# A hybrid diffusion layer on one core: one early dot in the last head, value blocks ahead of the last gate set, a modulation block behind the first two turns

## What is computed

```python
s1 = jnp.einsum('nhc,hkc->nhk', q[:, :, 0], p['sub_keys'][0]); s2 = ...   # 8 heads, 128 keys each
v1, i1 = lax.top_k(s1, TOPK); v2, i2 = lax.top_k(s2, TOPK)                # TOPK = 16
top_s, pos = lax.top_k(cand, TOPK); idx = ...; gates = softmax(top_s)
act = gelu(einsum('nd,nhkd->nhk', xb, expert_u[ib]))
out = einsum('nhk,nhkd->nd', act * gb, expert_v[ib])
```

## Time and profile before

| | us |
|---|---|
| median of 3 executions | 2940.51 (2938.43 to 2943.66) |
| profiled execution, its time | 2936.83 |
| its span, first to last instruction | 2935.0 |
| PE busy | 2807.2 (96%) |
| DVE busy | 2178.6 (74%) |
| ACT busy | 1224.7 (42%) |
| POOL busy | 968.8 (33%) |

### The profile page before, as it was taken

One profiled execution on the slowest core, in us unless ns is written; L12 is line 12 of the kernel. 1 busy time (PEld: TensorE's weight loads), 2 busy tenths in 40 slices (PEclk: granted clock), 3 DMA queues, 4 the chain that ended last, 5 costly groups with the idle time before them and its releaser, 6 DMA issues.

```text
span 2935.0 us, 59432 instructions
## 1 busy us (share of the span) xinstructions
PE 2807.2 (96%) x24142; PEld 2477.1 (84%) x24142; DVE 2178.6 (74%) x3107; ACT 1224.7 (42%) x1889; POOL 968.8 (33%) x626
## 2 busy tenths in 40 slices
PE   6999999999999989899989999999999999999998
PEld 4999999677777869799989888888888887777776
DVE  3245553666666653579998999988888989999988
ACT  3333333333333343353336666654444434343333
POOL 0001101122222220049883444431114444444442
PEclk8999999799999989999999999999999999999999
DMA  9633332343341045557779999999999999999997
GB/s 404 264 122 129 123 132 77 134 149 121 127 143 67 5 174 182 183 205 268 251 251 339 360 397 395 393 389 417 417 401 418 417 418 418 418 417 418 417 418 311
DMA packets 205973, 813.66 MB, mean 277 GB/s; under 512 B 81328, under 2 KB 99888, under 8 KB 116688
## 3 DMA queue, kind: packets, MB, share of 16 engines
q1 hardware_dynamic: 103312, 525.61, 46.9%
q0 software_dynamic: 36864, 268.45, 22.1%
q10 hardware_dynamic: 65600, 16.78, 2.5%
HBM read 771.45 MB, written 39.32 MB: 276 GB/s over the span
## 4 chain that ended last, share of the span: by engine, by line
PE 25%; DMA 13%; DVE 12%; issue 5%; SPq 1%; ACT 1%; another core or an unknown queue 0%; DVEq 0%; ACTq 0%
DMA work<-act_table 13%; PE ps L2121 12%; PE ps L2126 6%; PE ps L2474 2%; DVE x L2674 2%; DVE work L2800 2%; DVE wlo L2805 2%; DVE ps L2614 1%; DVE ps L2606 1%; DVE work L2608 1%; PE ps L2525 1%; PE ps L2519 1%; PE ps L2518 1%; DVE work L2646 0%; PE ps L2109 0%
## 5 line engine op out<-in xcount | busy, mean ns | idle before, releaser
L2562 POOL DMA_INDIRECT work<-expert_v,idx x128 | 341.2, 2666 | 378.1 <-DVE work L2800 360.6
L2518 PE MATMUL ps<-whi,hboth 128*128 128x512 f32 x1024 | 399.5, 390 | 6.2 <-ACT whi L2329 6.2
L2121 PE MATMUL ps<-hboth,whi 128*128 128x512 f32 x1664 | 403.4, 394 | 0.0
L2519 PE MATMUL ps<-whi,hboth 128*128 128x512 f32 x1024 | 399.3, 390 | 0.0
L2562 POOL DMA_INDIRECT x<-u_rows,idx x128 | 245.5, 1918 | 437.3 <-DVE x L2674 254.7
L2121 PEld LDWEIGHTS ps<-hboth,whi 128*128 128x128 f32 x1664 | 305.2, 188 | 60.5
L2800 DVE SCALAR_TENSOR_TENSOR work<-work,dots 128x2048 f32<-128x2048 f32 x127 | 297.8, 2345 | 2.3 <-DMA work<-expert_v,idx 2.2
L2525 PE MATMUL ps<-wlo,hboth 128*128 128x512 f32 x1024 | 255.7, 392 | 15.3 <-DVE wlo L2805 15.3
L2525 PEld LDWEIGHTS ps<-wlo,hboth 128*128 128x128 f32 x1024 | 190.6, 188 | 62.6 <-DVE wlo L2805 23.6
L268 PE MATMUL ps<-hhi,whi 128*128 128x384 f32 x704 | 236.2, 335 | 0.0
L270 PE MATMUL ps<-hhi,wlo 128*128 128x384 f32 x704 | 235.2, 334 | 0.0
(11 more groups left out here) (425 smaller groups left out, 5977.2 us busy)
## 6 DMA issues: line engine op xcount, KB each, us to landing
raw<-expert_u SPq DMA_DIRECT2D x85, 1024.0 KB, 8.0
work<-expert_v SPq DMA_DIRECT2D x64, 1024.0 KB, 15.0
raw<-expert_v SPq DMA_DIRECT2D x64, 1024.0 KB, 15.0
raw<-w_in SPq DMA_DIRECT2D x50, 1024.0 KB, 4.8
x<-w_ada SPq DMA_DIRECT2D x48, 1024.0 KB, 5.4
raw_more<-expert_u SPq DMA_DIRECT2D x43, 1024.0 KB, 7.8
z<-w_ada SPq DMA_DIRECT2D x42, 1024.0 KB, 10.4
raw<-w_out SPq DMA_DIRECT2D x16, 1024.0 KB, 4.8
```

The lines of the kernel that those rows point to most:

```text
L2121: pe.matmul(both, whi[:, r, k, :], hboth[:, :, k, CTX:T], start=(k == 0), stop=False)
L2518: pe.matmul(bank, ah, vh[:, part], start=first, stop=False)
L2519: pe.matmul(bank, al, vh[:, part], start=False, stop=False)
L2562: nc.gpsimd.indirect_dma_start(out=buf, out_offset=None, in_=rows, in_offset=bass.IndirectOffsetOnAxis(ap=idx[:, s:s + 1], axis=0)).then_i ...
```

## The change

Three places are edited.

1. In the scan pairs the early modulation slot 3 no longer stands ahead of the last score step; it stands behind `turn_first(1)`. ACT's copy of the sums moves behind its copy of the second turned group.
2. In the heads there are 19 early dots in place of 21: head 7 has one in place of three. The scatter stage has 69 in place of 67. POOL issues one gather behind the low part of each of three blocks (m = 9, 10, 11 and so on), where it issued three behind the first.
3. `done_tok` is placed ahead of `vg`, so that it lies under `stage[0]`. SP waits for the stores of `stage[0]` alone, loads the value blocks 0 and 1, and only then waits for the stores of `stage[1]` and loads the first set.

```diff
                 def one(it, more):
-                    ada_copy(it, 0)
                     for g in range(GR):
                         turned.wait(act, it, g + 1)
                         if g == 2:
                             ada_sums(it, 0)
                         tn_ready.inc(nc.scalar.activation(tn[:, g], ...))
+                        if g == 1:
+                            ada_copy(it, 0)
...
                         if n >= 2:
-                            ada(it, n - 2)
+                            if n - 2 < ADA_EARLY - 1:
+                                ada(it, n - 2)
                             scores_masked.wait(pe, it, 2 * n - 2)
...
                     turn_first(0)
                     turn_first(1)
+                    ada(it, ADA_EARLY - 1)
                     scores_masked.wait(pe, it, 12)
...
-        EARLY_DOTS = DOTS_PER_HEAD * (PKH - 1)
+        EARLY_DOTS = DOTS_PER_HEAD * (PKH - 2) + 1
...
         accs = carve(fb_, D)
+        done_tok = carve(fb_, 2, D)
         vg = [carve(fb_, D) for _ in range(4)]
-        done_tok = carve(fb_, 2, D)
...
                 load_fixed(M_DOWN - 1)
+                sp.wait_ge(stage_out[0].sem, 16 * (SETS // 2))
+                load_v(expert_v[0], 0)
+                load_v(expert_v[1], 1)
+                sp.wait_ge(stage_out[1].sem, 16 * (SETS // 2))
                 for r in range(2):
-                    sp.wait_ge(stage_out[r].sem, 16 * (SETS // 2))
                     sp.wait_ge(spilled[r].sem, 16 * 2)
                 groups(0, 0)
-                load_v(expert_v[0], 0)
-                load_v(expert_v[1], 1)
                 groups(1, 2)
...
-                        for s in range(DOTS_PER_HEAD * (h - 1), DOTS_PER_HEAD * h):
-                            pool.wait_ge(idx_ready.sem, s // TOPK + 1)
-                            gather_u(s)
+                    s = DOTS_PER_HEAD * (h - 1) + (m - 1) % PER_HEAD
+                    if 1 <= h < PKH and (m - 1) % PER_HEAD < DOTS_PER_HEAD and s < EARLY_DOTS:
+                        pool.wait_ge(idx_ready.sem, s // TOPK + 1)
+                        gather_u(s)
...
-                    for s in range(DOTS_PER_HEAD * (h - 1), DOTS_PER_HEAD * h):
+                    for s in range(DOTS_PER_HEAD * (h - 1), min(DOTS_PER_HEAD * h, EARLY_DOTS)):
                         dot(s)
```

More of the change, by code:

```diff
@@ L2012, in build_program @@
         accs = carve(fb_, D)
+        done_tok = carve(fb_, 2, D)
+        assert fb_[0] == NK * GT
         vg = [carve(fb_, D) for _ in range(4)]
-        done_tok = carve(fb_, 2, D)
         v_raw = [done_tok[:, r].rearrange("p (k c) -> p k c", k=KD) for r in range(2)] + [raw[:, 0], raw[:, 1]]
```

## The result

The changed kernel takes 2923.25 us (median of 4 runs, 2923.11 to 2927.75) against 2942.09 for the kernel before in the same measurement (4 runs): a ratio of 0.9938, 95% interval 0.9922 to 0.9955. A second measurement on another chip gave 0.9950 (0.9937 to 0.9963). So the change is worth 15 to 19 us. The forecast was 5.7, and the range's lower end, 2927, was not low enough. The two profiled executions are only 13.7 us apart: that of before lies 5.3 us under the median of its four, that of the changed kernel 0.1 under its own.

The account below looks back on a forecast made before the run. PE was taken to set the up stage and DMA bytes the down stage. Edits of -3.4, -2.0 and -0.3 summed to -5.7 us, so 2934.8 us against a median of 2940.5; range 2927 to 2942.

Parts of the forecast that it names:

- Edit 1, -3.4: Scan pairs: PE's 0.57 us wait for the last masks goes in each of six pairs, 3.4 us together.
- PE does the same work in another order: Scan pairs: reordered PE reaches the sums at 630.33, later than the masks, so only its 0.57 us idle time goes.
- Edit 2, -2.0: Heads and scatter stage: gate turns 3.9 us earlier, scatter stage 3.0, less 1 us for dot 19; bounds -8.7 and +4.
- (a): Head 1: the third gather, now behind a later low part, lands late; its dot loses 5 to 7 us on DVE.
- (b): Heads 2 and 3: about half of the contention between dots and POOL's low parts goes, -4 us.
- (c): Heads 4 to 6: the low part meets each third dot, 2.2 us less 0.7 from the first dot; +4.5 us in all.
- rival 1: Head stage gives all it has: PE's 7.6 us wait and 1.1 of its start go; -12.4 us, 2928.1; chance 0.22.
- 2.2 us either way: Heads 4 to 6: a dot meeting a low part costs 2.2 us more, whichever of the two comes first.
- Edit 3, -0.3: Handover to the down stage: bytes bind, only 0.45 us of DMA time to be won; bounds -4 and +6.
- the rival that the store slips beside the value blocks: Handover: the last table store slips and DVE stands at the first set; 2947 in the middle, 2952 at most; chance 0.08.
- Up to 4 us of slip PE's old wait covers: Handover: without ACT's 4.20 us wait the down start is about 2189 against 2193.07, leaving 4 us for a late store.
- lands near 2176: Handover: by the skill's turns rule the last table store lands near 2176 beside the value blocks; Edit 3 would give -0.45.

Follow-up runs that it names:

- h2: The changed kernel with value blocks 2 and 3 also loaded ahead of the wait for the last table store; 2927.0 us, 0.9957 of the kernel before.
- c3: The changed kernel with the last store's first rows stored apart and only 64 of 128 rows in the first two table stores; 2925.7 us, 0.9951 of before.
- c2: The changed kernel with only the first 64 of 128 rows stored in the first two table stores; 2924.0 us, 0.9946 of the kernel before.
- c1: Edits 1 and 2 on the kernel before, with only 64 of 128 rows stored in the first two table stores; 2923.6 us, 0.9943 of before.
- e12_no_handover: Edits 1 and 2 on the kernel before, without edit 3; 2924.9 us, 0.9951 of the kernel before.
- after_again: The changed kernel, all three edits, measured once more; 2925.5 us, 0.9950 of the kernel before.
- e12_again: Edits 1 and 2 without edit 3, measured again beside the changed kernel on one chip; 2923.8 us, 0.9942 of the kernel before.
- e2: Edit 2 alone on the kernel before; 2929.2 us, 0.9962 of the kernel before.
- h1: The changed kernel with the last table store in two, the first gate sets' rows apart with their own semaphore; 2929.3 us, 0.9963 of the kernel before.

## Why the prediction was wrong, point by point

**Edit 1, -3.4: right in its mechanism, too small.** The 0.57 us waits went, in all six pairs. The step that failed is "PE does the same work in another order": the same matmuls cost PE 0.27 us less per pair in the new order. 0.84 x 6 = 5.0 us, which is what the edit alone measured (-5.0); the 6.4 us between the means of the traces hold the variation of the scan stage as well.

**Edit 2, -2.0: this is where the forecast broke.** Its parts can be read from the starts of the first dots, against the 6.1 us by which the heads begin earlier. (a) was a little short: the third dot waits 7.3 us for its gather, and head 2 begins 8.0 late, where the sum had 6. (b), "about half of that contention goes", was too little: heads 2 and 3 take back 3.1 and 3.7 us, where the sum had 4 for both; head 2's first dot, 4.04 us, had been contended as well, and the sum did not count it. (c) failed outright: "the low part follows at once, so that it meets the third dot: 4.48 - 2.28 = 2.2 us in each". It does meet it, and the dot pays nothing, because the dot had begun first. Heads 4 to 6 gave -1.2 us (the first dot of head 4, 2.49 instead of 3.66) and not +4.5. The forecast had +6.5 us for DVE at head 7 where the trace has 0; the turns then came 9.1 us sooner behind the heads' first matmul, not 3.9. The 9.1 are PE's wait (7.63 less 0.72), its waits for POOL's low parts near 1508 (3.0 us before, 1.1 now), and 0.2 in small. Another 1.5 us came behind the turns, where PE's six matmuls take 272 to 300 ns instead of 421 to 448: the granted clock is 1.00 (the upper level) from 1519 to 1539, and was 0.83 in the mean from 1525 to 1545 in the kernel before, where PE had just stood for 7.6 us. That is rival 1 nearly word for word, at 0.22.

By the Trainium skill, "SBUF — State Buffer", section "Who interferes with whom", the two engines exclude each other for a whole instruction, and the prediction worked out -2.1 us for the three heads by that rule, for a low part that comes second, beside its own +4.5. The changed kernel gave -1.2. Its trace and the kernel with the low parts in quarters agree with the rule (3.37 us for a dot that meets 1.30 us pieces). I had a number by which to choose: the low parts of 4.46 us in the earlier trace rows are 2.40 plus nearly a whole dot of 2.28, which turns explain and a shared rate does not explain better; and I took "2.2 us either way".

**What no step had.** Two more gathers in the scatter stage bring the landing of the first table store from 99.9 us to 105 to 120, past the 104.4 us after which its buffer is wanted. The prediction spoke only of the last store, at the handover. Some executions lose 10 us by it.

**Edit 3, -0.3.** That bytes bind the down stage was right, and so was the rival that the store slips beside the value blocks; the 0.08 for it was too low, although the price was not 2947. The slip is 11 us (209.6 to 220.4; 209 to 213 in the traces without edit 3, 219 to 220 in those with it as it stands and without a long wait of ACT). The failed step is "Up to 4 us of slip PE's old wait covers", which looked at PE only. What the slip moves is the DMA work that stands behind the store: on SP's queue the set and value blocks 2 and 3, on POOL's the gathers of value rows (8.8 us). DMA time of 5.9 us was lost where 2.7 was lost before. SP's share is not the whole: in h2 the value blocks stood ahead of the wait and in c3 the sets did not wait for the store either, and 5.7 and 5.0 us were lost all the same, while POOL stood 12.5 and 15.0 us. No run lets POOL go ahead, so its share is argued and not shown. The Trainium skill's rule on turns, from "DMA: Bandwidth & Descriptors", section "Queues, rings and completion order", led me to "lands near 2176"; the store's lateness by 11 us says that turns beside value blocks are slower turns, so the rule gave no bound. By pairs of traces the edit costs 1.4 to 4.0 us from the last up product on (c2 against c1, the edit alone, the changed kernel against e12_no_handover). By the times it costs 3.8 us alone (0.05 to 0.29%), and 0.4 and 1.7 us on top of the others, which these runs can't tell from nothing. In part that is the long wait of ACT: where it delays PE, the last store has landed before it is wanted, and after_again and e12_again take 730.2 and 732.1 us to the end, edit 3 or not. The rest stays open.

**The chances.** Faster by over 0.2% had 0.49 and came out. Two errors of the same sign, in (b) and (c), and the 0.27 of edit 1 outweighed what edit 3 cost and made the sum too small by 8.0 us against the profiled execution (5.7 for 13.7). That alone would have ended at the range's edge: 2936.8 - 13.7 + 3.7 is 2926.8. The rest of the miss is the 3.7 us that the sum added for the median; here the median lay 0.1 above the profiled execution.

## What to carry to other kernels

Where two engines exclude each other, ask which instruction is issued first: the one that is already running loses nothing, and the other waits for all that is left of it. A long instruction on the engine with slack is then the costly one. Cutting it into pieces halved the price of one meeting here, from 2.2 to 1.1 us, but made more of them, and the time did not change. Before an order is changed, look at what is only just in time, above all a store whose buffer is used again; here a margin of 5 us out of 105 turned into a wait that is long only in some executions, so that one profile of each kernel is not enough. In a stage that runs by bytes, follow every queue that waits for the same event, and not the compute engines: here SP's and POOL's both stood for one store, and moving two blocks of SP's ahead of the wait left the hole as large as it was.

## What the hardware showed that I had not expected

An engine that issues a DMA can stand in the issue itself. ACT's table store takes 0.38 to 0.44 us to issue as a rule, and 5.9 to 12.1 us in six places of four traces (e2, after_again, e12_again, h1; 6.82 and 9.02 in e12_again, 10.57 in after_again, where the issue ended 114.7 us behind the start of the one before it). In each of these the store before was still under way. That is not enough for it: in the changed kernel the third store lands 18.7 us after the fourth is issued, in 0.38 us. What decides is not shown. With 4 MB in pieces of 256 bytes the store got 20 GB/s beside a full load of large transfers, and value blocks beside its tail made it 10.8 us longer with 2 MB and 14.6 with 4.
